# Own buffers for the first two weight units behind each projection and norm of a three-layer network, and the next two split behind the norm

## What is computed

```python
# first block, at the end of its mixing part
x = x + rms_norm(merged @ w_out, norm_mix_post)
h = rms_norm(x, norm_ffn_pre)
x = x + rms_norm((silu(h @ w_gate) * (h @ w_up)) @ w_down, norm_ffn_post)

# second block
x = x + rms_norm(merged @ w_out, g_mix_post)
h = rms_norm(x, g_mem_pre)
q = h @ w_mem_q                      # then softmax(q k^T) v, 4 heads, 256 memory keys
x = x + rms_norm(o @ w_mem_o, g_mem_post)
h = rms_norm(x, g_ffn_pre)
f_gate, f_up = split(h @ w_ffn_in)
x = x + rms_norm((silu(f_gate) * f_up) @ w_ffn_out, g_ffn_post)
```

## Time and profile before

| | us |
|---|---|
| median of 3 runs | 2979.09 |
| lowest and highest of the 3 | 2977.27, 2981.9 |
| the profiled execution, a run of its own | 2981.74 |
| its span, from first to last instruction | 2979.9 |
| PE busy in it | 2826.6 (95%) |
| PE weight loads | 2236.6 (75%) |
| DVE busy | 1519.9 (51%) |
| ACT busy | 1077.5 (36%) |
| POOL busy | 446.4 (15%) |
| mean granted clock of TensorE | 0.975 of full speed |

### The profile page before, as it was taken

One profiled execution on the slowest core, in us unless ns is written; L12 is line 12 of the kernel. 1 busy time (PEld: TensorE's weight loads), 2 busy tenths in 40 slices (PEclk: granted clock), 3 DMA queues, 4 the chain that ended last, 5 costly groups with the idle time before them and its releaser, 6 DMA issues. The chain is left out here.

```text
span 2979.9 us, 36682 instructions
## 1 busy us (share of the span) xinstructions
PE 2826.6 (95%) x13172; PEld 2236.6 (75%) x13172; DVE 1519.9 (51%) x2343; ACT 1077.5 (36%) x1713; POOL 446.4 (15%) x319
## 2 busy tenths in 40 slices
PE   5999999999999899999999999989998899899998
PEld 4874678888887687467888888767686588688886
DVE  5556673533324656667353333455588635643423
ACT  4345333422224534533342222443623324532221
POOL 1010111311102201011121110220101112211101
PEclk9999999999999899999999999999997899999999
DMA  3320012222222232001222222212231122122232
GB/s 130 125 88 29 29 58 86 84 99 96 101 100 99 75 118 85 29 29 57 96 75 99 98 100 99 99 59 83 77 121 57 43 85 71 57 85 94 90 112 85
DMA packets 37056, 245.92 MB, mean 83 GB/s; under 512 B 4144, under 2 KB 5168, under 8 KB 7984
## 3 DMA queue, kind: packets, MB, share of 16 engines
q1 hardware_dynamic: 33600, 239.09, 22.8%
q10 hardware_dynamic: 3312, 4.93, 0.5%
HBM read 241.91 MB, written 2.10 MB: 82 GB/s over the span
## 5 line engine op out<-in xcount | busy, mean ns | idle before, releaser
L529 PE MATMUL bank<-h_hi,w_hi 128*128 128x512 f32 (+1 forms) x2280 | 884.7, 388 | 22.6 <-DVE w_lo L1466 10.6
L531 PE MATMUL bank<-h_hi,w_lo 128*128 128x512 f32 (+1 forms) x2280 | 866.0, 380 | 0.0
L530 PE MATMUL bank<-h_lo,w_hi 128*128 128x512 f32 (+1 forms) x2280 | 865.8, 380 | 0.0
L1466 DVE TENSOR_TENSOR w_lo<-raw,w_hi 128x2048 fp32r<-128x2048 f32 x223 | 515.2, 2311 | 532.1 <-ACT w_hi L1011 373.6
L529 PEld LDWEIGHTS bank<-h_hi,w_hi 128*128 128x128 f32 x2280 | 432.2, 190 | 118.5 <-issue 30.6
L531 PEld LDWEIGHTS bank<-h_hi,w_lo 128*128 128x128 f32 x2280 | 432.1, 189 | 81.1
L530 PEld LDWEIGHTS bank<-h_lo,w_hi 128*128 128x128 f32 x2280 | 432.4, 190 | 79.2 <-issue 3.6
L1011 ACT ACTIVATE w_hi<-raw 128x2048 fp32r<-128x2048 f32 x141 | 269.3, 1910 | 225.0 <-PE bank L531 218.4
L529 PE MATMUL bank<-a_hi,w_hi 128*128 128x512 f32 x528 | 205.7, 390 | 0.0
L531 PE MATMUL bank<-a_hi,w_lo 128*128 128x512 f32 x528 | 205.7, 390 | 0.0
L530 PE MATMUL bank<-a_lo,w_hi 128*128 128x512 f32 x528 | 205.7, 390 | 0.0
(11 more groups left out here) (383 smaller groups left out, 4166.9 us busy)
## 6 DMA issues: line engine op xcount, KB each, us to landing
raw<-in_stream SPq DMA_DIRECT2D x226, 1024.0 KB, 4.9
x<-in_xT SPq DMA_DIRECT2D x2, 1024.0 KB, 12.6
out_T<-x ACTq DMA_DIRECT2D x8, 256.0 KB, 2.1
p_f<-in_pT ACTq DMA_DIRECT2D x2, 512.0 KB, 3.9
memf<-in_memT ACTq DMA_DIRECT2D x1, 1024.0 KB, 5.5
cst_sb<-in_cst ACTq DMA_DIRECT2D x1, 411.5 KB, 6.6
pos_i<-in_pos ACTq DMA_DIRECT2D x1, 258.0 KB, 9.2
vec<-in_vec ACTq DMA_DIRECT2D x2, 26.0 KB, 1.7
```

The lines of the kernel that those rows point to most:

```text
L529: nc.tensor.matmul(ps, wh, xh, start=start, stop=False)
L530: nc.tensor.matmul(ps, wh, xl, start=False, stop=False)
L531: return nc.tensor.matmul(ps, wl, xh, start=False, stop=stop)
L1466: nc.vector.tensor_tensor(w_lo[s][:, :], raw[s][:, :], w_hi[s][:, :].bitcast(F32), ALU.subtract).then_inc(lo_ready, 1)
```

## The change

Three things are changed.

**Buffers.** Units 0 and 1 of `gu` in both blocks, and of `mq`, get a high and a low buffer of their own (`EARLY`) in an arena whose tensors are dead at that point; the tile `mq` moves from offset 0 to 32 to make room. `home` says which buffers a unit has, and `first_units` on PE reads them from there. For these units ACT's `split_unit` no longer waits for PE to finish the unit two before. The two `raw` buffers stay as they are.

**Order in the projection.** With four units the first call now stands behind tile 1, the next two behind tile 3, and the last behind `half_squares` of tile 4 on ACT and behind the copies of tiles 4 and 5 on DVE. With two units they stand behind tile 1 and tile 3. None is left inside the chains of the halves.

**The next two units.** Their high parts are made by ACT right behind the root for half 0 of the next norm, which itself moves from the middle of half 1's chain to its end; their wait (the first two entries of `HALVED` for `mq` and `gu`) is now for the last tiles of the projection. DVE makes the low parts of both `mo` units behind half 0 of `mq`; of the two `gu` units it makes one behind half 0 of `first_units` and the other, as before, behind the first products.

```diff
-    "mq": [3, 4],
-    "gu": [3, 4] + [2 * p + 2 for p in range(2, KF)],
+    "mq": [-1, 0],
+    "gu": [-1, 0] + [2 * p + 2 for p in range(2, KF)],
...
-        mq = ar("mq", 0, [4, S])
+        mq = ar("mq", 32, [4, S])
...
+        EARLY = {
+            (1, "gu"): [early("gu1_0", 0, 8), early("gu1_1", 16, 56)],
+            (2, "mq"): [early("mq_0", 16, 24), early("mq_1", 83, 0)],
+            (2, "gu"): [early("gu2_0", 0, 8), early("gu2_1", 16, 24)],
+        }
+
+        def home(c, v):
+
+            block = 1 if c.base is BASE1 else 2
+            for (b, st), two in EARLY.items():
+                u = v - c.base[st]["U"] if b == block else -1
+                if 0 <= u < 2:
+                    return two[u]
+            return w_hi[v % 2], w_lo[v % 2]
...
-                                mm = mac(ps[:, cols(g)], (u0 + p) % 2, 8 * g + k, P, h_hi[:, k, at], h_lo[:, k, at],
-                                         k == 0 and g == 0, k == KD - 1 and g == 1)
+                                b = slice((8 * g + k) * P, (8 * g + k + 1) * P)
+                                mm = mac_at(ps[:, cols(g)], hi[:, b], lo[:, b], h_hi[:, k, at], h_lo[:, k, at],
+                                            k == 0 and g == 0, k == KD - 1 and g == 1)
...
-                kind, n = releases(st)[u]
-                act.wait_ge(tile_done if kind == "T" else part_done, c.at(kind, st, n))
+                if not is_early(c, v):
+                    kind, n = releases(st)[u]
+                    act.wait_ge(tile_done if kind == "T" else part_done, c.at(kind, st, n))
...
                 for n in range(4):
                     squares_of_psum(c, st, n)
-                    if n == 3 or n == 1 and units == 4:
-                        split_unit(c, st, n // 2 if units == 4 else 0)
+                    if n == 1:
+                        split_unit(c, st, 0)
+                    elif n == 3:
+                        for u in range(1, max(units - 1, 2)):
+                            split_unit(c, st, u)
                 half_squares(c, st, 4)
+                if units == 4:
+                    split_unit(c, st, 3)
                 half_squares(c, st, 5)
                 half_root(c, st, 0, 3, HALF_RSTD[0][:, 0:HALF])
                 for m in range(KD):
                     raw_half(c, norm_st, which, after, 0, m)
                     if m == 2:
                         half_squares(c, st, 6)
-                        if units == 4:
-                            split_unit(c, st, 2)
                 half_squares(c, st, 7)
                 half_root(c, st, 1, 6, HALF_RSTD[1][:, 0:HALF])
-                split_unit(c, st, units - 1)
                 for m in range(KD):
                     raw_half(c, norm_st, which, after, 1, m)
-                    if m == 1:
-                        half_root(c, norm_st, 0, 2, rstd[:, 0, cols(0)])
+                half_root(c, norm_st, 0, 2, rstd[:, 0, cols(0)])
+                for u in range(2):
+                    split_unit(c, "gu" if norm_st == "norm2" else "mq", u)
                 half_root(c, norm_st, 1, 4, rstd[:, 0, cols(1)])
```

More of the change, by code:

```diff
@@ L372, in block_kernel, with early, is_early @@
         om_lo = ar("om_lo", 58, [4, S], F32R)
+        def early(name, hi, lo):
+            return ar(f"{name}_hi", hi, [UC], F32R), ar(f"{name}_lo", lo, [UC], F32R)
+        EARLY = {
[10 more added lines that the diff above has]
+            return w_hi[v % 2], w_lo[v % 2]
+        def is_early(c, v):
+            return home(c, v)[0] is not w_hi[v % 2]
         bank = [ctx.enter_context(nc.psum_tensor(f"bank{i}", [P, S], F32)) for i in range(8)]
@@ L745, in first_units @@
                         ps = free_bank(c, st, 2 * half + p)
+                        hi, lo = home(c, u0 + p)
                         for k in range(KD):
@@ L1010, in split_unit @@
                 else:
-                    nc.scalar.activation(w_hi[v % 2][:, :], raw[v % 2][:, :], ACT.Copy).then_inc(hi_ready, 1)
+                    nc.scalar.activation(home(c, v)[0][:, :], raw[v % 2][:, :], ACT.Copy).then_inc(hi_ready, 1)
             def stage_loop(c, st, evac):
@@ L1190, in gate_up @@
                 act.preload_act_table(ACT.Silu)
-                split_unit(c, st, 0)
                 act.wait_ge(tile_free, c.at("T", st, 4))
@@ L1194, in gate_up @@
                     nc.scalar.activation(sg[:, p, :], sg[:, p, :], ACT.Silu).then_inc(act_took, 1)
-                split_unit(c, st, 1)
                 for p in range(2):
@@ L1414, in _ @@
             project_norm(c, "wout", "post1", 2, "normh")
-            for u in range(2):
-                split_unit(c, "mq", u)
             attention(c, "mem")
@@ L1453, in split_unit @@
                 else:
-                    low_part(v % 2)
+                    hi, lo = home(c, v)
+                    nc.vector.tensor_tensor(lo[:, :], raw[v % 2][:, :], hi[:, :].bitcast(F32), ALU.subtract).then_inc(lo_ready, 1)
                 if c.base is BASE1 and 0 <= v + 1 - c.base["bm"]["U"] < KD:
@@ L1592, in project_norm @@
                             half_out(c, st, 6)
-                            if units == 4:
-                                split_unit(c, st, 2)
-                        if half == 1 and m == 1:
-                            split_unit(c, st, units - 1)
                 add_squares(c, norm_st, 1)
@@ L1700, in gate_up @@
                         nc.vector.tensor_tensor(res[:, p, cols(half)], ps[:, cols(1)], rstd[:, 0, cols(half)], ALU.mult).then_inc(tile_free, 1)
-                        if half == 1 and p == 0:
-                            split_unit(c, st, 0)
+                    if half == 0:
+                        split_unit(c, st, 0)
                 dve.wait_ge(tile_free, c.at("T", st, 4))
@@ L2046, in _ @@
                     ins.then_inc(tile_free, 1)
-            for u in range(2):
-                split_unit(c, "mq", u)
+                if half == 0:
+                    for u in range(2):
+                        split_unit(c, "mq", u)
             attention(c, "mem")
```

## The result

| | median us | lowest, highest | runs |
|---|---|---|---|
| before, beside the changed kernel | 2980.49 | 2977.27, 2982.55 | 4 |
| changed | 2960.39 | 2957.67, 2962.3 | 4 |

The account below looks back on a forecast made before the run. PE bounds the kernel, busy 2826.6 of 2979.9 us. Terms 5.2, 6.8, 7.8 and 3.9 sum to 23.7 us: 2958.0 from the profiled execution, 2955.4 as median, stated as 2956, range 2949 to 2966.

Parts of the forecast that it names:

- 1.65 and 1.28: Layer 0: PE's waits for the squares of tile 7 and for the low part of gu unit 1, both to go.
- 2.28: Layers 0 and 1: PE's wait for the low part of gu unit 2, to go in each.
- the margin at tile 5: Half 0's chain: the squares of tile 5 still end before PE asks for them, with 0.1 us to spare.
- two pieces: Squares and start of half 0's chain: low part ahead of the first scaling, 0.8 us later; ACT's high part, 0.3 us.
- Layer 0: Three PE waits go, 1.65 + 1.28 + 2.28 = 5.2 us, with no clock gain counted.
- Layer 1: The same three waits, 5.2 us, plus 1.6 us for a stretch at 1.2 GHz: 6.8 us.
- `wout` to `mem`: Second block: squares 1.70, low part 1.2, wait at mem 3.7 and clock at mem 1.2, together 7.8 us.
- `mo` to `gu`: Second block: wait for gu unit 2 of 2.25 and clock of 1.6 go, 3.9 us; squares' 3.1 us stay.
- The rival on the clock: Stretches at 1.2 GHz come at other places, so the 4.4 us of clock are lost: 2960 to 2962; chance 0.14.
- Half 0's chain: Rival: the chain stays late, PE waits for squares about as before, 5 us lost, 2961; chance 0.15.
- the second pair: Rival: splits of the next two units come late, waits before gu unit 2 and at mem stay: 2970; chance 0.08.
- The slower side's rule: Rival: squares of tile 5 queue behind a late load, each us beyond slack idles PE at three places; chance 0.03.

Follow-up runs that it names:

- first pair only: Changed kernel with the splits of the next two units put back in gate_up and in front of the attention mem: 2969.0 us, ratio 0.9968 to before.
- later sum: Changed kernel, but behind mo PE sums the squares for half 1 after the sixth feature tile of gu unit 0, not the second: 2958.26 us, ratio 0.9918.
- eight more: Changed kernel with eight useless matmuls of 512 columns behind first_units in each of layers 0 and 1: 2958.37 us, ratio 0.9917 to before.
- later sum and four: Changed kernel with the half 1 sum behind mo moved later and four useless matmuls in each of layers 0 and 1: 2953.83 us, ratio 0.9913.
- four more again: Changed kernel with four useless matmuls behind first_units in each of layers 0 and 1, run a second time: 2961.91 us; first time 2958.16.
- the split put ahead: Changed kernel, but ACT splits the second early unit ahead of the squares of tile 4 instead of behind them: 2964.42 us, ratio 0.9942.

## Why the prediction was right, and where it was off

2955.4 came out of the sum, 2956 was said, 2960.39 was measured: inside the range of 2949 to 2966, 4.4 us over, with two errors of opposite sign. The waits were understood; that the number came so near is in part luck, since the places gave 2.7 us more than was said and other stages took 4 to 7 back.

*The waits.* Right one by one. 1.65 and 1.28 went and came back alone with the old places of the first pair; 2.28 with those of the second. No new wait took their place in layers 0 and 1. The chain started 0.7 us late where 0.9 was said, the squares of tile 7 came 2.5 earlier where 2.0 was said, and the margin at tile 5 was 0.27 us instead of 0.1. The prediction had two pieces there, 0.8 for the low part and 0.3 for ACT (which together would be 1.1, not 0.9); only the first one counted, since ACT's root came 1.06 us behind PE's sum over the squares in both kernels.

*The terms.* Layer 0: 5.2 said, 6.0 measured. Layer 1: 6.8 and 7.6. Both lack the same 0.8: a wait was priced at its idle time alone, and each costs another 0.26. `wout` to `mem`: 7.8 and 8.0: idle time fell by 12.84 - 6.87 = 6.0 where 1.70 + 1.2 + 3.7 = 6.6 was said (the third item of `mem` still waits 0.87 us), matmuls by 2.0 where 1.2 was, and two waits at 0.26 account for half a us of it. `mo` to `gu`: 3.9 and 4.8: idle time fell by 6.22 - 3.99 = 2.2, as said, matmuls by 2.6 where I had 1.6 of clock. The rest of that is again 0.26 for the wait, and the stretch at 0.5 behind the wait for squares that stays: 6.8 us long from 2594.06 in the first execution of before, 3.4 in its second one and in the changed kernel. The edit at `mo` itself, its first pair, gave nothing and cost nothing, as said: the 3.1 us for squares stay, and an 0.85 in front of the sum for half 1 stands in both kernels.

*The clock.* The three stretches at 0.5 behind the waits for `gu` unit 2 (one in layer 0 or 1, one in the second block) and behind the one at `mem` went in all three executions of the changed kernel. The price of 1.6 us is shown by the kernel before, whose stretch sits in layer 0 or in layer 1; that of 1.2 at `mem` by the first pair only. The Trainium skill, "TensorE: Matmul & The Clock Gate", Part 1, says that the throttled state is the default and that activity releases it. From that sentence alone the prediction read that equal waits cost the same; in either execution of before one place of two paid, so the rows do not agree with that reading, and the prediction was right to take 1.6 for two of the three places and not for all. The gain at `mem` is less safe than it looks: in four of the kernels above, edited elsewhere, C has one or two stretches at 0.5 without that wait (123.0 us for the later sum, 124.6 for eight more, for later sum and four, and for four more again), up to 3.4 us of slower matmuls.

*The step that failed* is one that isn't in the sum: that all other stages keep their lengths. The rival on the clock had the mechanism, stretches that come at other places, but as the loss of the gain at the edited places. That gain came in full, and N1 and N2, 400 us behind the edits, lost 1.9 to 3.2 and 1.0 to 1.5 us. This accounts for 3 to 4.7 of the 4.1 to 6.6 us between the places' 26.4 and the 20 to 22 measured. The rest lies in stages that scatter without any edit, above all the start of layer 0: the first wait for `mid_lo` ended between 61.4 and 65.7 us in these traces. Why it scatters is open. So is why N1's distance follows the time taken before it: that it does was forecast and met with four and eight more, the reason was not tested.

*The other rivals.* Half 0's chain did not make PE wait and the second pair came in time in all three executions. The slower side's rule, a us of idle PE for each us of lateness, was confirmed by the split put ahead; in the changed kernel no load came that late. Reading weights from the new buffers costs nothing: in A all matmuls have the pace they had, 93.92 us for 598 of them, and those with `gu_hi` follow at the 0.12 us of the others.

## What to carry to other kernels

When a split, copy or conversion for the next stage stands inside a chain that several engines pass around, give its output a buffer in memory that is free at that point and move it ahead of the chain or behind it; here the buffer alone brought nothing. Price a removed wait at its idle time and a little more (0.26 us here) for the overlap of matmuls that is lost on both sides of it, and look at what stands behind the moved instruction's own load. Then compare stage by stage with repeated traces: when the places gain what they should and the total less, look at the clock in stages with little work before looking for a fault in the edit.

## What was not expected of the hardware

A program's place against the stretches at 1.2 GHz can repeat from run to run to some tenths of a us (4.55, 4.72 and 4.56 us behind N1's first sums in the changed kernel, 3.88 and 3.65 with four more matmuls; but 2.32 and 3.72 in the kernel before), and shortening one stage shifts it in a later one: N1 took 33.0 to 36.3 us with the same instructions, by where the lower clock began (1.5 to 4.7 us behind those sums). 1.8 or 3.7 us of useless matmuls, 0.9 or 1.8 in each layer, did not show in the total.

A wait costs PE more than its idle time at full clock as well, measured as 0.78 us for three in layer 0: 0.16 us because the matmul ahead of it overlaps with none, and 0.10 us at the first one behind it.
